# Four row buffers for the probabilities of the odd attention, and the merge of a pair of maps ahead of the next maximum

## The reference, cut to what matters

```python
def diff_attend(q, kvs, lam):
    scale = q.shape[-1] ** -0.5
    ss = [jnp.einsum('bhiqd,bhikd->bhiqk', q, k, preferred_element_type=jnp.float32) * scale for k, _ in kvs]
    ps = joint_softmax(ss)
    out = None
    for p, (_, v) in zip(ps, kvs):
        a = (p[:, :, 0] - lam * p[:, :, 1]).astype(v.dtype)
...
```

## Time and profile before

| | |
|---|---|
| median of 3 runs | 2794.43 us (2794.01 to 2795.34) |
| profiled execution, its own time | 2790.57 us |
| its span | 2788.8 us |
| mean granted clock of TensorE | 0.974 |
| TensorE busy | 2654.2 us (95%) |
| VectorE busy | 1833.8 us (66%) |
| ScalarE busy | 1449.2 us (52%) |
| chain that ended last | TensorE 84%, VectorE 7%, ScalarE 3% |

### The profile page before, as it was taken

How to read it: one execution, slowest core, us unless ns; L and a number is a source line. 1 busy time by engine, 2 the same in 40 slices (tenths; PEclk the granted TensorE clock), 3 DMA queues, 4 the chain that set the end, 5 groups by cost and what they waited for, 6 DMA issues and landing times.

```text
span 2788.8 us, 33741 instructions
## 1 busy us (share of the span) xinstructions
PE 2654.2 (95%) x12853; PEld 2206.0 (79%) x12853; DVE 1833.8 (66%) x2322; ACT 1449.2 (52%) x2063; POOL 180.8 (6%) x226
## 2 busy tenths in 40 slices
PE   7999899999999789999999899998999999998998
PEld 5777678888885578888888788877788788777787
DVE  6676677787786555556788656588756656546555
ACT  6564354544463344446777545665445545553553
POOL 2011000000060000000000000002100100100100
PEclk9999999999999879999999999999999999999999
DMA  8673166776660046557999556440364655650444
GB/s 299 230 249 113 61 234 219 250 261 229 226 192 16 0 165 199 185 186 248 328 319 324 211 159 218 155 163 1 114 203 166 202 174 178 205 188 5 158 157 145
DMA packets 260767, 511.40 MB, mean 183 GB/s; under 512 B 9769, under 2 KB 40705, under 8 KB 260496
## 3 DMA queue, kind: packets, MB, share of 16 engines
q1 hardware_dynamic: 256576, 498.11, 53.3%
q0 software_dynamic: 4048, 11.36, 1.3%
HBM read 507.33 MB, written 1.05 MB: 182 GB/s over the span
## 4 chain that ended last, share of the span: by engine, by line
PE 84%; DVE 7%; ACT 3%; DMA 2%; issue 2%; POOL 1%; SPq 0%; DVEq 0%; ACTq 0%; POOLq 0%
PE bank L422 23%; PE bank L423 23%; PE bank L426 23%; PE bank L1438 2%; PE bank L1451 2%; DVE h_hid L2912 1%; PE bank L393 1%; PE bank L1466 1%; ACT whi L326 1%; PE bank L394 1%; PE bank L395 1%; DVE wlo L330 1%; PE bank L541 1%; DMA raw<-in_moe_w 1%; PE bank L1440 1%
## 5 line engine op out<-in xcount | busy, mean ns | idle before, releaser
L330 DVE TENSOR_TENSOR wlo<-raw,whi 128x1024 fp32r<-128x1024 f32 (+1 forms) x964 | 1141.9, 1199 | 664.3 <-ACT whi L326 658.3
L326 ACT ACTIVATE whi<-raw 128x1024 fp32r<-128x1024 f32 (+1 forms) x964 | 987.2, 1035 | 781.9 <-PE bank L426 727.9
L422 PE MATMUL bank<-whi,xhi 128*128 128x512 f32 (+2 forms) x2320 | 882.9, 381 | 21.0 <-issue 12.7
L426 PE MATMUL bank<-whi,xlo 128*128 128x512 f32 (+2 forms) x2320 | 873.5, 377 | 0.0
L423 PE MATMUL bank<-wlo,xhi 128*128 128x512 f32 (+2 forms) x2320 | 872.6, 376 | 0.0
L422 PEld LDWEIGHTS bank<-whi,xhi 128*128 128x128 f32 x2320 | 438.8, 189 | 101.7 <-issue 20.3
L426 PEld LDWEIGHTS bank<-whi,xlo 128*128 128x128 f32 x2320 | 438.1, 189 | 76.6
L423 PEld LDWEIGHTS bank<-wlo,xhi 128*128 128x128 f32 x2320 | 439.0, 189 | 74.5 <-issue 0.5
L422 PE MATMUL bank<-whi,f_hhi 128*128 128x512 f32 x496 | 194.0, 391 | 0.0
L426 PE MATMUL bank<-whi,f_hlo 128*128 128x512 f32 x496 | 193.1, 389 | 0.0
L423 PE MATMUL bank<-wlo,f_hhi 128*128 128x512 f32 x496 | 193.1, 389 | 0.0
(11 more groups left out here) (573 smaller groups left out, 2796.2 us busy)
## 6 DMA issues: line engine op xcount, KB each, us to landing
raw<-in_ffn_w SPq DMA_DIRECT2D x180, 1024.0 KB, 5.1
raw<-in_moe_w SPq DMA_DIRECT2D x96, 1024.0 KB, 6.5
raw<-in_moe_w SPq DMA_DIRECT2D x48, 768.0 KB, 4.9
raw<-in_ada_w SPq DMA_DIRECT2D x24, 1024.0 KB, 5.4
raw<-in_ev_w_in SPq DMA_DIRECT2D x24, 1024.0 KB, 5.8
raw<-in_ffn_w SPq DMA_DIRECT2D x36, 512.0 KB, 3.7
raw<-in_hyb_w_in SPq DMA_DIRECT2D x18, 1024.0 KB, 5.1
raw<-in_attn_w_qkv SPq DMA_DIRECT2D x18, 1024.0 KB, 5.1
```

What stands on the lines that cost most here:

```text
L326: nc.scalar.activation(whole, part, ACT.Copy).then_inc(sem("w_hi"), 1)
L330: nc.vector.tensor_tensor(wlo[s][:, 0:rows, 0:n], part, whole.bitcast(F32), ALU.subtract)\
L422: nc.tensor.matmul(bank[:, 0:n], xk_h, whi[s][:, wk, 0:n], start=first, stop=False)
L426: ins = nc.tensor.matmul(bank[:, 0:n], xk_l, whi[s][:, wk, 0:n], start=False, stop=last)
```

## The change

The odd attention gets four row buffers in place of two: the two of before and the first 512 columns of both halves of the tile `sq` (o_sq in the traces), which holds squares in an earlier stage. The other attentions keep two. The exponential of item i then waits for what item i-4 has to finish. In VectorE's program the merge of pair k stands before the maximum of the item that follows, and no longer behind it; copies of single items stay behind the maximum.

```diff
-    def attn_pe(e, base, items, ready, *deps, turn=None, aside=None, tb=None):
+    def attn_pe(e, base, items, ready, *deps, turn=None, aside=None, tb=None, rows=prob):
...
-                ins = nc.tensor.transpose(PT[u % 2][:, k * P:k * P + P], prob[i % 2][:, k * P:k * P + P], ident)
+                ins = nc.tensor.transpose(PT[u % 2][:, k * P:k * P + P], rows[i % len(rows)][:, k * P:k * P + P], ident)
...
         for i, it in enumerate(items):
+            if i >= 1 and items[i - 1].get("pair"):
+                items[i - 1]["merge"](e, i - 1)
             e.eng.wait_ge(sem("scores"), base + i + 1)
...
-            if i >= 1:
-                former = items[i - 1]
-                if former.get("pair"):
-                    former["merge"](e, i - 1)
-                elif not former.get("lead"):
-                    take(i - 1)
+            if i >= 1 and not items[i - 1].get("pair") and not items[i - 1].get("lead"):
+                take(i - 1)
...
-    def attn_act(e, base, items, also=None, tb=None):
+    def attn_act(e, base, items, also=None, tb=None, rows=prob):
...
-            if i >= 2:
-                if items[i - 2].get("lead"):
-
-                    e.after(f"merged{i - 1}")
+            held = i - len(rows)
+            if held >= 0:
+                if items[held].get("lead"):
+
+                    e.after(f"merged{held + 1}")
                 else:
-                    e.eng.wait_ge(sem("prob_turned"), tb + place[i - 2] + 1)
-            nc.scalar.activation(prob[i % 2][:, 0:it["n"]], SC[i % 2][:, 0:it["n"]], ACT.Exp,
+                    e.eng.wait_ge(sem("prob_turned"), tb + place[held] + 1)
+            nc.scalar.activation(rows[i % len(rows)][:, 0:it["n"]], SC[i % 2][:, 0:it["n"]], ACT.Exp,
...
-        own, other = prob[(i - 1) % 2], prob[i % 2]
+        own, other = rows4[(i - 1) % 4], rows4[i % 4]
...
+    rows4 = prob + [sq[:, t, 0:N] for t in range(NT)]
...
-                attn_act(e, ATT0[2], W_ITEMS + D_ITEMS, lambda i: odd_also_act(e, i))
+                attn_act(e, ATT0[2], W_ITEMS + D_ITEMS, lambda i: odd_also_act(e, i), rows=rows4)
...
-                attn_pe(e, ATT0[2], W_ITEMS + D_ITEMS, odd_ready, "ckT", "qoT1", "band", aside=odd_aside_pe)
+                attn_pe(e, ATT0[2], W_ITEMS + D_ITEMS, odd_ready, "ckT", "qoT1", "band", aside=odd_aside_pe,
+                        rows=rows4)
```

## The result

| | before | changed |
|---|---|---|
| median of 5 runs, same chip | 2794.43 us (2794.01 to 2797.47) | 2779.69 us (2778.70 to 2785.56) |
| profiled execution | 2790.57 us | 2778.70 us |
| its span | 2788.8 us | 2776.9 us |
| granted clock of TensorE | 0.974 | 0.977 |
| TensorE busy | 2654.2 us | 2649.1 us |

The ratio is 0.9948, with a 95% interval of 0.9936 to 0.9960: 14.7 us faster by the medians. So the direction was right and the size wrong.

A forecast was written before the change was run, and what follows sets the result against it. It took the differential half to be bound by a serial chain through each merge, 5.39 us a pair. Low-clock gain 3.7 plus three quarters of 8.7 made 10.2, off 2794.4: 2784.2 us, range 2781.5 to 2791.0.

The forecast's parts named there:

- (a): Window half of the odd attention and the other attentions: TensorE never idles or nothing changes there, so gain 0.
- (b, c): Differential half: VectorE's merge moves before the next pair's first maximum, and exponentials no longer wait for merges; 3.43 us a pair.
- The ring: Differential half, VectorE and ScalarE: exponential, reciprocal, merge, maximum, two exponentials in a closed cycle, 3.43 us a pair.
- the cover of the casts: VectorE, pairs 4 and 5: casts behind the second maximum end before the reciprocal is due; cost 0, otherwise a tenth or two.
- the 21.4 us: Differential half: ScalarE's exponentials wait this long in 7 places for a merge, because two buffers are reused.
- three quarters of the way: Differential half: gain put between low and high TensorE clock, 3.7 + 0.75 x 8.7 = 10.2 us.
- high-clock case: Differential half with TensorE at its higher clock from pair 3 on: last transposes 10.7 us earlier, total gain 12.4 us.
- the drain: End of the odd attention: last transposes and 16 output products take 2.44 us at the higher clock, 1.7 us gained.
- (d): Behind the attention: everything hangs on the last output products, so the whole gain, 10.2 us, reaches the end.
- Clock stays low: Rival: TensorE holds its lower level throughout the differential half; gain only 3.7 us, 2790.7 us; chance 0.11.
- Swallowed downstream: Rival: the stage after the attention begins no earlier, so no gain, 2794.4 us; chance 0.05.
- Slower, as the score products no longer overlap: Rival, differential half: a pair's two score products run in sequence at low clock, 6.94 us a pair, 2805.3 us; chance 0.04.

The follow-up runs named there:

- order_only: The kernel before with the merge moved ahead of the next pair's first maximum, but still two row buffers: 2777.50 us, ratio 0.9934; repeated, 2781.47 us, 0.9946.

## Why the prediction was right in its direction and too small

**(a) Window items, other attentions: 0.** Right: 46.00 us again, TensorE busy 44.3 by the records (some are missing: 230 against 239).

**(b, c) The ring.** Right in kind, and 0.1 us too long. The first merges are 3.32 apart, 3.43 was forecast: from the exponential of the second map to the reciprocal it is 0.80 and not 0.88 (ScalarE 912.84, VectorE 913.64), and between the two exponentials 0.68 and not 0.72 (912.16, 912.84). At the pairs with work between the maxima the distances are 4.02 and 4.23, forecast 4.00 and 4.22. VectorE of the changed kernel shows where the schedule starts, and the first ring:

```profile
901.29 0.16 DVE L1912 RECIPROCAL vtop<-den 128x1 f32<-128x1 f32 x1
...
901.75 0.75 DVE L1916 SCALAR_TENSOR_TENSOR tmp<-tmp,vtop 128x512 f32<-128x512 f32 x1
...
904.62 0.16 DVE L1912 RECIPROCAL vtop<-den 128x1 f32<-128x1 f32 x1 [0.92 <-ACT o_sq L1554]
...
905.07 0.75 DVE L1916 SCALAR_TENSOR_TENSOR o_sq<-o_sq,vtop 128x512 f32<-128x512 f32 x1
```

With the free VectorE at 901.29 in place of 899.57, 1.72 is to be taken off: the second merge stands at 903.35 (forecast 903.45), and the last transposes at 928.18 (forecast 928.44 for the high clock). At pairs 4 and 5 the cover of the casts was gone, as the prediction allowed ("where that cover fails, a tenth or two"): the chain runs over L1363, and the 3.37 is VectorE's own work. What the prediction ascribed to the buffers, that the exponentials no longer wait for merge k, was not a gain of its own: order_only has it without them. The prediction never costed the two halves of the change apart, and its reading of the 21.4 us pointed at the half that is worth nothing.

**The clock.** "I take three quarters of the way" was right for the middle: from pair 3 on the transposes take 0.66 and the ring holds. From VectorE's release to the end of the last outputs the gain is 43.68 - 32.32 = 11.4. The high-clock case was 12.4; the drain stayed at the lower level for most of its length (0.66 + 3.06 in place of 2.44, so 1.3 less), and the ring gave back 0.3. The stage's mean of 0.85 is seven tenths of the time at the higher level, close to the three quarters assumed, but the lower level lies in the first pairs, where the high-clock schedule has it too (up to 908.68), and in the drain, so it cost little of the gain: the 10.2 were 1.2 short. The kernel before idled 1.6 us a pair ahead of the transposes, 2.1 at most, and had 0.63 to 0.76 over 42 to 45 us; with these gaps filled it had 1.00.

**(d) "So the gain is carried to the end."** This is the step that failed. The gain was carried, and something was added to it, since the stages behind do not have one fixed time: the router's stage hangs on TensorE's level, which differs from execution to execution (13.2 to 16.9 with the same instructions) and with what the kernel did before. The working held it for a constant. Added up, with the averages of the profiles: 11.3 for the stage, 0.6 for the first merge, which starts 0.46 behind VectorE's release in place of 1.05, 2.1 for the router's stage, less 0.4 for the stretch ahead of it, make 13.6. The mean spans of the same nine profiles are 13.8 apart (2791.6 and 2777.8). By the medians 14.7, 13.7 and 16.5 were measured. Of the 4.5 us that the forecast lacked, 1.2 are the clock inside the stage, 0.5 are that the stage in the one profile read (42.38) was that much shorter than its mean (42.84), and 1.7 lie behind the attention; the 1.1 that are left are inside the spread of the medians and have no row.

**The median and the range.** The sum was made against an execution of 2790.57 and taken off the median, with 0.5 us for the spread. One kernel's executions lie up to 14 us apart (2790.57 to 2804.44 for the one before, over several chips), and 42.38 for the stage was on the low side of its mean, 42.84. The low end needed these terms: 12.4 for the high clock, 0.5 for the stage's own spread, and up to 3.6 (16.86 - 13.24) for a stage behind whose level can change, so about 2778. The row for it was there: TensorE idle for 6.5 us ahead of the router's transposes, all of them at the lower level.

**The rivals.** Clock stays low: no, 0.85, which is also the figure that the prediction wanted to see exceeded. Swallowed downstream: no. Slower, as the score products no longer overlap: they overlap less, as was worked out. At the high clock the second begins 0.60 after the first (weight loads at 916.38 and 916.98; 0.72 was forecast) and the two take 1.72 (1.77); where the exponentials of pair 6 are 1.29 apart it begins 1.22 after, and the two take 2.35, one behind the other. But the ring is the longer one in both places, and no pair took 6.94.

What stays open: how TensorE's clock at the end of the attention reaches the router's stage over 31 us of work in between, although the two go together in all fourteen profiles; and where the rest of the spread of single executions lies, for 2790.57 and 2793.82 have nearly the same two stretches.

## What to carry to other kernels

A wait that is named many times in a profile need not be what holds the kernel: before a buffer is doubled, ask whether the thing waited for could itself be earlier, by following the chain around one full period, and try the reorder by itself. When TensorE idles a microsecond or two in each turn of a loop, price the loop at both levels of its clock; here 7.8 us came from filling the gaps alone, with the order left as it was. A few dummy products in the wait measure that in one run, as long as they end with the wait: the 12 at pair 1 and the 48 ahead of the router ran past it and delayed what stood behind. Where the clock decides, untouched stages with an idle time ahead of them belong in the range, and the range comes from several profiles of the kernel before.

## What the runs showed of the hardware

- In this loop short gaps kept the clock down. With TensorE busy 29 to 32 of 42 to 45 us, with an idle time of 1.6 us a pair on average and 2.1 at most, the granted clock was 0.63 to 0.76; with dummy products in the gaps 1.00, and the stage 7.8 us shorter. The level went up and down from pair to pair: four transposes took 1.12, 0.66, 1.12 and 0.66 us in pairs 1 to 4. The Trainium skill ("TensorE: Matmul & The Clock Gate", "A second HAM failure mode: psum-queue depth-cycling") tells of a kernel whose short idles between groups of products make the clock switch back and forth; the trace agrees. The prediction had no row for the price of a gap.
- Dummy products are cheap but not free: 16 records of 128x128 take 1.98 us at the high clock, 0.124 each, and 96 took 10.72, 0.112 each.
- A copy of 128x512 in fp32 from SBUF to SBUF took 0.43 us on VectorE, and 0.34 from its start to the next one's; the merge, with two tensors, took 0.75 and 0.67. The Trainium skill ("VectorE: DVE Perf Modes", "The perf-mode tier table (the rule you actually need)") gives such a copy twice the rate of `tensor_tensor`; the merge, which reads two tensors as well, took twice the copy's time from start to start.
- Score products that contract over 64 rows each overlap as far as they are started together. In the timeline one takes 1.12 us, two that start together 1.13, and two of which the second starts 0.60 after the first 1.72. TensorE's timeline of the changed kernel:

```profile
916.38 1.72 PE L1438 MATMUL bank<-o_kT,o_qT 64*128 64x512 f32 x4
918.28 0.66 PE L1466 MATMUL bank<-kb,tmp 128*128 128x128 f32 x4 [0.17 <-DVE tmp L1916]
```
